# A two-block network on one core: another order of the attention tail's filler work, norms 4 and 6 scaled in halves

## The reference

```
for i in range(2):                                   # first block
    x = x + 0.5 * swiglu(rms_norm(x, ffn1_norm[i]), ...)      # d_ff = 2816
    h = rms_norm(x, mix_norm[i])
    x = x + (moba_mixer(h, ...) if i == 0 else mamba2_mixer(h, ...))
    x = x + 0.5 * swiglu(rms_norm(x, ffn2_norm[i]), ...)
# second block
mod = silu(c) @ w_ada + b_ada;  shift, scale, gate = split(mod, 3)
h = rms_norm(x, norm_g) * (1.0 + scale) + shift
proj = h @ w_in                                      # 9216 columns
m = sigmoid(ga) * hgrn2_part(proj) + sigmoid(gb) * retention_part(proj)
x = x + gate * (m @ w_out)
return rms_norm(x, final_g)
```

## Time and profile before

| | |
|---|---|
| median of 3 runs | 1431.44 us (1428.26 to 1435.96) |
| the profiled execution | 1428.24 us, span of the trace 1426.4 us |
| PE busy | 1381.5 us, 97% |
| DVE busy | 887.2 us, 62% |
| ACT busy | 705.3 us, 49% |
| POOL busy | 305.0 us, 21% |
| mean granted TensorE clock | 0.991 of full speed |
| w_lo split (L390) on DVE | 220 times, mean 2.46 us |
| w_hi split (L382) on ACT | 220 times, mean 1.92 us |
| load of half a unit of w_in, issue to landing | 4.6 us |

### The profile page before, as it was taken

The page is one execution under the profiler, slowest core; times in us unless marked ns, Lnnn a source line. Parts: engine busy times, 40 slices in busy tenths (PEclk is TensorE's granted clock), DMA queues, the critical chain, the costliest instruction groups (busy, mean ns, idle before and its releaser), DMA issues.

```text
span 1426.4 us, 18571 instructions
## 1 busy us (share of the span) xinstructions
PE 1381.5 (97%) x7113; PEld 1168.1 (82%) x7113; DVE 887.2 (62%) x922; ACT 705.3 (49%) x813; POOL 305.0 (21%) x238
## 2 busy tenths in 40 slices
PE   9999999989999999999899999999999999999996
PEld 7888888768888888888799888878788898888785
DVE  5544569654544564544588988556866647666475
ACT  6444355645344454434467668454443546456443
POOL 3200002000000000000000153059991103318430
PEclk9999999989999999999999999999999999999999
DMA  9555555425556555655445652597765355444240
GB/s 294 195 177 191 191 177 177 148 89 177 177 186 196 177 179 181 198 184 195 127 143 184 226 183 95 179 375 268 265 220 192 111 187 177 148 147 148 89 148 30
DMA packets 158282, 254.27 MB, mean 178 GB/s; under 512 B 8784, under 2 KB 99232, under 8 KB 156560
## 3 DMA queue, kind: packets, MB, share of 16 engines
q1 hardware_dynamic: 155136, 232.94, 50.1%
q0 software_dynamic: 2576, 18.45, 3.5%
q10 hardware_dynamic: 512, 2.08, 0.4%
HBM read 252.35 MB, written 1.08 MB: 178 GB/s over the span
## 4 chain that ended last, share of the span: by engine, by line
PE 88%; DVE 5%; ACT 3%; issue 2%; DMA 1%; POOL 0%; SPq 0%; ACTq 0%; POOLq 0%; DVEq 0%
PE psum L607 10%; PE psum L609 10%; PE psum L608 10%; PE psum L642 5%; PE psum L644 5%; PE psum L643 5%; PE psum L1780 3%; PE psum L1781 3%; PE psum L1782 3%; PE psum L449 3%; PE psum L451 3%; PE psum L450 3%; PE psum L428 3%; PE psum L430 3%; PE psum L429 3%; DVE w_lo L390 2%
## 5 line engine op out<-in xcount | busy, mean ns | idle before, releaser
L390 DVE TENSOR_TENSOR w_lo<-raw,w_hi 128x2048 fp32r<-128x2048 f32 x220 | 540.8, 2462 | 353.7 <-ACT w_hi L382 353.6
L382 ACT ACTIVATE w_hi<-raw 128x2048 fp32r<-128x2048 f32 x220 | 421.2, 1915 | 363.3 <-PE psum L609 124.6
L607 PE MATMUL psum<-w_hi,hT_hi 128*128 128x512 f32 x704 | 279.3, 397 | 2.8 <-DVE w_lo L390 2.1
L609 PE MATMUL psum<-w_hi,hT_lo 128*128 128x512 f32 x704 | 275.3, 391 | 0.0
L608 PE MATMUL psum<-w_lo,hT_hi 128*128 128x512 f32 x704 | 274.9, 391 | 0.0
L607 PEld LDWEIGHTS psum<-w_hi,hT_hi 128*128 128x128 f32 x704 | 132.7, 188 | 31.3 <-DVE w_lo L390 3.6
L609 PEld LDWEIGHTS psum<-w_hi,hT_lo 128*128 128x128 f32 x704 | 132.5, 188 | 28.4
L608 PEld LDWEIGHTS psum<-w_lo,hT_hi 128*128 128x128 f32 x704 | 132.7, 188 | 26.5
L503 POOL TENSOR_TENSOR meansq<-sumsq 128x2 f32<-128x2 f32 x7 | 4.1, 592 | 702.3 <-ACT xn L474 702.3
L642 PE MATMUL psum<-w_hi,hidT_hi 128*128 128x512 f32 x320 | 125.0, 391 | 1.6 <-DVE hid L721 1.6
L644 PE MATMUL psum<-w_hi,hidT_lo 128*128 128x512 f32 x320 | 124.7, 390 | 0.0
(11 more groups left out here) (375 smaller groups left out, 2206.5 us busy)
## 6 DMA issues: line engine op xcount, KB each, us to landing
raw<-in_ffn_w_down SPq DMA_DIRECT2D x88, 512.0 KB, 4.3
raw<-in_ffn_w_gate SPq DMA_DIRECT2D x87, 512.0 KB, 4.0
raw<-in_ffn_w_up SPq DMA_DIRECT2D x87, 512.0 KB, 4.9
raw<-in_w_in SPq DMA_DIRECT2D x72, 512.0 KB, 4.6
raw<-in_ssm_w_in SPq DMA_DIRECT2D x48, 512.0 KB, 4.7
raw<-in_attn_w_qkv SPq DMA_DIRECT2D x24, 512.0 KB, 4.7
ada_in<-in_w_ada POOLq DMA_DIRECT2D x8, 1536.0 KB, 8.8
raw<-in_ssm_w_out SPq DMA_DIRECT2D x16, 512.0 KB, 4.6
```

The lines of the kernel that those rows point to most:

```text
L382: act.activation(w_hi[:, slot, :], raw[:, slot, :], ACT.Copy).then_inc(sem("hi_ready"), 1)
L390: dve.tensor_tensor(w_lo[:, slot, :], raw[:, slot, :], w_hi[:, slot, :].bitcast(F32), ALU.subtract)\
L607: pe.matmul(to, a, hi[:, kk, :], start=k == 0, stop=False)
L609: m = pe.matmul(to, b, hi[:, kk, :], start=False, stop=k == KD - 1)
```

## The change

1. **Attention's filler.** A table `fill` says which tiles (j, k) PE does in each slot. The first tiles of slots 5 to 8 stay with wo+0 and wo+1, but in another order, wo+0 is used up in slot 7, and the last tiles are (3,5), (2,7), (3,6), (3,7). The split of wo+3 moves from behind slot 8 to behind slot 7 on ACT and DVE.
2. **DVE and ACT in the qkv part.** `prob_dve` stands before `rope_dve`. An activation on one column at i == 6 loads the Exp table before the first exponentials.
3. **Norm 2.** The split of ffn2_0's second unit goes from between the two adds of x to behind the first four `hT_lo`.
4. **Norms 4 and 6.** xn is written in two halves of 512, with one semaphore for each token tile. The early split moves behind four `hT_lo`.
5. **Norm 4.** PE does 14 matmuls into a free bank in front of the transposes.
6. **Norm 6.** ACT modulates tiles 2, 3, 6 and 7, DVE the others. POOL clears `hg_att` only when hT is complete.
7. Some semaphores are merged into others with higher counts.

```
@@ norm_act
-                act.activation(xn[:, 1, :], x[:, 1, :], ACT.Copy, scale=rstd[:, 1:2]).then_inc(sem("xn"), 1)
+                for cs in HALVES:
+                    act.activation(xn[:, 1, cs], x[:, 1, cs], ACT.Copy, scale=rstd[:, 1:2]).then_inc(sem("xn_1"), 1)
@@ norm_dve
             if not deferred:
+                dve.wait_ge(sem("rstd"), n + 1)
+                for cs in HALVES:
+                    dve.tensor_scalar(xn[:, 0, cs], x[:, 0, cs], rstd[:, 0:1], None, ALU.mult).then_inc(sem("xn_0"), 1)
+            if gain:
+                hT_lo_tiles(dve, n, gain, range(4))
                 for unit in early:
                     split_lo(dve, unit)
-                dve.wait_ge(sem("rstd"), n + 1)
-                dve.tensor_scalar(xn[:, 0, :], x[:, 0, :], rstd[:, 0:1], None, ALU.mult).then_inc(sem("xn"), 1)
-            if gain:
-                hT_lo_tiles(dve, n, gain, range(4))
-                if deferred:
-                    for unit in early:
-                        split_lo(dve, unit)
                 hT_lo_tiles(dve, n, gain, range(4, KD))
@@ norm_pe
-                            pe.wait_ge(sem("xn"), xn_before + TT)
+                            pe.wait_ge(sem(f"xn_{t}"), xn_before + k // 4 + 1)
@@ attn_pe
-            for slot in range(12 - FIRST_SLOT, HEAD_SLOTS):
-                k = slot - (12 - FIRST_SLOT)
-                wo_tiles(2 * (k // 4), (k,))
-                wo_tiles(2 * (k // 4) + 1, (k,))
+            fill = {5: ((0, 0), (0, 1)), 6: ((1, 0), (0, 2)), 7: ((1, 1), (0, 3)), 8: ((1, 2), (1, 3)),
+                    9: ((2, 4), (2, 5)), 10: ((2, 6), (3, 4)), 11: ((3, 5), (2, 7), (3, 6), (3, 7))}
+            for slot in range(12 - FIRST_SLOT, HEAD_SLOTS + 1):
+                for j, k in fill[slot]:
+                    wo_tile(j, k)
                 head_slot_pe(pe, slot)
-            for j in (2, 3):
-                wo_tiles(j, (6,))
-            for j in (2, 3):
-                wo_tiles(j, (7,))
@@ attn_act
+                if i == FIRST_SLOT - 1:
+                    act.activation(table_use[:, :], ident[:, 0:1], ACT.Exp)
                 head_slot_act(act, i - FIRST_SLOT)
...
-                if slot == 8:
+                if slot == 7:
                     split_hi(act, u + SLOTS)
@@ attn_dve
+                prob_dve(dve, i - FIRST_SLOT)
                 if i % 2 == 0 and 1 <= c <= ROPED:
                     rope_dve(dve, c - 1)
-                prob_dve(dve, i - FIRST_SLOT)
...
-                if slot == 8:
+                if slot == 7:
                     split_lo(dve, u + SLOTS)
             split_lo(dve, u + 1 + SLOTS)
             for h in range(2):
-                if h:
-                    split_lo(dve, u + 2 + SLOTS)
@@ ssm_pe
+            keep_busy(pe, BUSY_BEFORE_XN)
             norm_pe(pe, 4, False)
@@ second_act
+            def modulated(k):
+                act.wait_ge(sem("xT"), 6 * KD + (k | 1) + 1)
+                act.activation(h_tmp[:, k, :], turned_x(6, k), ACT.Identity, bias=mod_cols[:, k:k + 1],
+                               scale=gain2[:, k:k + 1]).then_inc(sem("h_act"), 1)
...
+            for k in (0, 4):
+                hi_of_h(k)
+                modulated(k + 2)
+                hi_of_h(k + 1)
+                modulated(k + 3)
+                hi_of_h(k + 2)
+                hi_of_h(k + 3)
@@ second_pool
             norm_pool(pool, 6)
+            pool.wait_ge(sem("hT"), 7 * KD)
             pool.memset(hg_att[:, :, :], 0.0).then_inc(sem("att_clear"), 1)
@@ second_dve
-            split_lo(dve, early)
             norm_dve(dve, 6, None, False)
...
+            modulated(0)
+            modulated(1)
             for k in range(KD):
...
+                if k == 2:
+                    modulated(4)
+                    modulated(5)
+                if k == 4:
+                    split_lo(dve, early)
+                second_dve_lo(dve, k)
@@ the program of VectorE
-            norm_dve(dve, 2, ("ffn2_norm", 0), True, second_and_third("ffn2_0")[1:])
+            norm_dve(dve, 2, ("ffn2_norm", 0), True, second_and_third("ffn2_0"))
```

More of the change, by code:

```diff
@@ L1004, in attn_pe, with wo_tile @@
             u = FIRST_UNIT["wo"]
[L1006 removed]
+            def wo_tile(j, k):
                 n = BY_ROWS[j][1]
                 hi, lo = use_unit(pe, u + j)
[L1010 to L1025 removed]
+                pe.wait_ge(sem("oT"), k + 1)
+                for t in range(TT):
+                    to = psum[:, pair_banks(n)[t], :]
+                    a, b = (o[:, k % 4, t * P:(t + 1) * P] for o in (oT_hi[k // 4], oT_lo[k // 4]))
+                    pe.matmul(to, a, hi[:, k % 4, :], start=k == 0, stop=False)
+                    pe.matmul(to, a, lo[:, k % 4, :], start=False, stop=False)
+                    m = pe.matmul(to, b, hi[:, k % 4, :], start=False, stop=k == HEADS - 1)
+                if k % 4 == 3:
+                    m.then_inc(sem("unit_used"), 1)
+            fill = {5: ((0, 0), (0, 1)), 6: ((1, 0), (0, 2)), 7: ((1, 1), (0, 3)), 8: ((1, 2), (1, 3)),
[3 more added lines that the diff above has]
+                    wo_tile(j, k)
                 head_slot_pe(pe, slot)
[L1027 to L1030 removed]
         def head_slot_pe(pe, slot):
```

56 lines of the change are left out of this document (23 added, 33 removed).

## The result

| | before | after |
|---|---|---|
| median beside one another | 1433.7 us (4 runs, 1428.3 to 1440.2) | 1417.8 us (4 runs, 1417.6 to 1421.5) |
| the profiled execution | 1428.24 us, span 1426.4 | 1417.86 us, span 1416.0 |

The ratio is 0.9895, with a 95% interval of 0.985 to 0.994: the change is faster, by some 1.1%. One later run of before took 2140.7 us at a mean clock of 0.602; no ratio here counts it. The forecast was 1417.4 us.

A forecast was written before the change was run, and what follows sets the result against it. TensorE, busy 97% of the span, was taken as the bound, so only its waits and half-clock work could be won: 7.7 + 3.2 + 3.1 = 14.0 us off 1428.24, plus 3.2 for the median, 1417.4 us; range 1411 to 1426.

The forecast's parts named there:

- tail: Attention tail up to ffn2_0: waits removed, new waits and the clock together gain 7.7 us.
- norm 4: Norm 4: split moved 1.2 us, xn in halves 0.5, PE kept busy 1.3 to 1.5; together 3.2 us gained.
- norm 6: Norm 6: split and memset moved, slow transposes end at 1127.5, first matmul there instead of 1130.58; 3.1 us gained.
- Slot 1: Attention slot 1: prob ahead of the rope ends PE's wait before head 0's transposes; 2.2 us saved.
- Slot 5: Attention slot 5: tile (0,1) waits for head 1's low half, 2.5 us idle, net cost 1.8 us.
- Slots 6 and 7: Attention slots 6 and 7: the low half comes in time with 0.9 us to spare; cost zero.
- rival (c): Slots 6 and 7 lack the spare 0.9 us, gaps and slow clock follow; 2.3 us slower, 1433.7; chance 0.03.
- Slots 8 to 11: Attention slots 8 to 11: the 4.3 us w_lo wait goes, new waits of 1.8 and 0.7 come; net gain 1.8.
- Into ffn2_0: From the last wo matmul to ffn2_0's first: 5.1 us becomes near 2.6, PE's wait for x goes; gain 2.5 us.
- The clock in the tail: Half-clock stretches behind two tail gaps: 4.7 us back, less 1.7 for one assumed fall of the clock.
- (a): Rival: the tail's new order trades waits and the clock falls three times; 8.3 us gained, 1423.1; chance 0.20.
- (b): Rival: in the norms the split does not cause the long mean-square step, norm 4's clock falls; about 1424; chance 0.12.

The follow-up runs named there:

- slot5_old: The changed kernel with one pair of tiles exchanged, (0,0) and (1,0) in slot 5 as before, (0,1) and (0,2) in slot 6: 1415.9 us, ratio 0.9863.
- split_early: The changed kernel with the w_lo split of the second unit back in front of xn in norms 4 and 6: 1422.9 us, one run.
- no_busy: The changed kernel without the 14 matmuls ahead of norm 4's transposes: 1415.9 us, one run.

## Why the prediction was right, and where it was not

**The sum.** From the two first traces: tail 318.16 - 310.76 + 0.24 = 7.6 to ffn2_0 and 1.6 more behind it, 9.2 us (forecast 7.7); norm 4 2.9 (3.2); norm 6 3.3 (3.1). Together 15.4 where 14.0 stood; the mamba stage took 4.4 us back in that trace, the rest of the program 0.3, and 0.24 is the later start: 10.4, the distance of the spans.

**Slot 1.** 2.2 forecast, 2.26 measured. **Slot 5.** The wait was 2.5 in the forecast and 2.47 in the trace, and its price of 1.8 us is what `slot5_old` won back. **Slots 6 and 7.** No idle time, so rival (c) never began. **Slots 8 to 11.** 4.30 us went, 1.71 and 0.70 came, a gain of 1.9 where 1.8 stood. **Into ffn2_0.** 2.79 us from the last wo matmul to the first of ffn2_0 (307.97 to 310.76), 2.6 forecast. The forecast's 5.1 for before was counted from 313.0, where the first transpose stands; from start to start (312.80 to 318.16) it is 5.36. So the gain was 2.57, 2.5 forecast.

**The clock in the tail** is the term that was mis-sized in the profiled execution: one fall assumed, none seen, so 1.7 us more. As a mean over executions the term was too large by less: three of eight traces with this wait show the fall, 0.6 us.

**Norm 4.** The split's 1.2 us is 1.22 by `split_early`. Keeping PE busy was put at 1.3 to 1.5 and is worth 0.90 in the stretch. The step that failed is the last one: from the first transpose to the first matmul I took 2.0 us, and it was 2.33 (686.63 to 688.96). What is left of the 2.87 us, 0.75, stands where 0.5 was put for xn in halves.

**Norm 6.** The size was right and the reason only half so. The split and the memset cost what was said (1.59 and 1.42 us undone). But the forecast had slow transposes set the end, 3.5 us behind the first of them, and here it failed. The steps of ScalarE and VectorE began when it said, 2.4 and 2.8 us behind the first transpose (1116.46 to 1118.87 and 1119.30). It took these for ready well before the transposes were; but the first matmul needs the low half's end, and the wait in front of it is for that (0.46 us on hT_lo, first matmul at 1119.87, 3.41 behind the first transpose, where the transposes themselves took 2.95). So the path goes through ScalarE's w_hi split, and where the transposes do set the end it is only 0.16 us later. The forecast named w_hi on ScalarE as one of the signs that would prove it wrong, and it occurred. That the size came out right all the same is luck: two paths happen to be nearly equal.

**The rest.** Nothing in the forecast spoke of the mamba stage. Taking the profiled execution of before as base was right for the sum, but this execution was among the best of its kernel in its clock: in the mamba stage it had no fall. All runs of before show how much that is: those with a mean clock of 0.991 took 1427.8 to 1428.5 us, those with 0.981 took 1441.0 to 1441.7, so 1.3 us for each 0.001. At the same 0.991 the changed kernel took 1421.2 and 1421.5. That is 7 us less, and the medians lie 13.5 to 15.9 apart, with a mean clock that rose from 0.985 to 0.988 (the median in each series of before) to 0.993. This isn't a division by cause, since the mean clock also counts half-clock time in which PE has to wait anyway, as in norm 6 of before. From the stages of the two first traces I estimate for the 15.4 us: 5.6 by the clock (3.0 and 1.7 behind the tail's two gaps, 0.9 at norm 4 by `no_busy`) and 9.8 by waits and work taken away. The 15.4 fits the medians; the forecast's 14.0 had less for the tail's clock.

That the median came out at 1417.8 against 1417.4 is luck in part: the gain beside one another was 15.9 us (13.5 in the next series) where 14.0 was forecast, and the median of before had meanwhile moved from 1431.4 to 1433.7. These two errors of about 2 us cancel.

**Rivals.** (a) had three falls; none came in the first trace, and at most one in the tail of each of the eight with this order from slot 5 on. (b) said the long mean-square step is not the split's doing; `split_early` refutes it. (c) is answered above.

## What to carry to other kernels

Where one engine works through an order of filler and dependent work, count for each piece how many steps lie between its producer and itself. The 4.9 us of waits in this tail went when the pieces were placed a step later and the split behind the work that they needed, and nothing was lost elsewhere in it. Where TensorE sets the pace a wait has two prices, its own time and perhaps a fall of the clock, and the second came in some executions only: compare stages by their own milestones, take a second trace of the unchanged kernel before blaming a change for a slow stretch, and quote a mean clock with each time.
